# Gated tiles of four feed-forward layers transposed by VectorE in 32 x 32 blocks instead of by TensorE

## The chip, the cores and the metric

One core of a Trainium2 chip. The time is the device time of one execution of the whole program, in microseconds (us). The kernel before was run three times: 1187.49 us median, 1187.45 to 1188.47.

## What is computed

Two transformer blocks in sequence over x of 256 tokens by 1024 features, all in float32. The first has a gated MLP mixer, a feed-forward layer, a chunked attention with relative bias and a second feed-forward layer; the second has a feed-forward layer, a mixer of sparse and stick-breaking attention, a cross attention to a memory, and a feed-forward layer. Four feed-forward layers (f0, f1, f2, f3 in the kernel) are what the change touches. Each is

```python
def _swiglu_ffn(x, g_norm, w_gate_up, w_down):
    h = _rms_norm(x, g_norm)
    gate, up = jnp.split(h @ w_gate_up, 2, axis=-1)
    return (jax.nn.silu(gate) * up) @ w_down
```

with 2816 hidden features, added to x (with factor 0.5 in f2 and f3).

## The kernel before

**Numbers.** Every float32 operand of the large products is kept as two fp32r parts, hi (a rounded copy) and lo (the rest), and a product is three matmuls, hi hi, hi lo, lo hi (helper `three`, L325 to L327).

**Weights.** They come from HBM in units of 128 x 2048 float32 (1 MB). SyncE's queue loads a unit into one of three raw buffers; the load of unit i waits until the unit i-3 has been split. ScalarE copies raw to `whi` (L1069), VectorE subtracts to `wlo` (L1530); the pair goes into one of six slots, and ScalarE waits until TensorE no longer uses the unit that had the slot. Both engines call this `split()`. A chunk takes three units: two of the gate and up weights, one of the down weights, in the order gate-up c (two units), down c-1.

**A feed-forward layer.** The hidden features go in 11 chunks c of 256, the tokens in two halves t of 128. A half chunk (c, t) is:

- TensorE: `project` "gu" (c, t): 24 matmuls of 512 columns into bank `GB[t]`, gate in columns 0 to 255, up in 256 to 511.
- ScalarE `gated`: `sil[t]` = silu(gate) (L1184). VectorE `gated`: `hid[t]` = up * rstd * sil (L1654), 128 tokens x 256 features.
- TensorE `turn_hid`: two transposes of 128 x 128 (L331) of `hid[t]` into PSUM bank `XB[t]`.
- ScalarE `hi` (L1099) and VectorE `lo` (L1589): the transposed tile from PSUM into `hT[t]`, parts hi and lo.
- TensorE `downs` (c, t): 12 matmuls of 512 columns with `hT[t]` as stationary operand, added up in two banks over all chunks.

TensorE's order in chunk c: gu (c, 0), turn (c-1, 1), downs (c-1, 0), gu (c, 1), turn (c, 0), downs (c-1, 1). The first chunk has no downs: gu (0, 0), gu (0, 1), turn (0, 0), gu (1, 0), turn (0, 1), downs (0, 0), gu (1, 1). `downs` (c, 0) waits for the unit of down weights, `downs` (c, t) for `lo` (c, t), and gu (c, t) for `hid` (c-1, t), since it overwrites the bank. After the last chunk come turn (10, 1), downs (10, 0), and the last sums.

VectorE's order (and ScalarE's, with `hi` for `lo`) in chunk c: gated (c, 0), lo (c-1, 1), gated (c, 1), lo (c, 0), then `at_chunk(c, False)`, which makes `counts[c]` splits (3 in most chunks, 4 in chunk 1 of f0, f1 and f3, 1 in chunk 10 of f0, f1 and f2, none in chunk 10 of f3). Behind gated (0, 0), `at_chunk(0, True)` makes `early` splits: on VectorE 1 in f0 and 2 in the others, on ScalarE 1. In f0, f1 and f3 the last of the early splits completes the gate and up weights of chunk 1; in f2 it is the down unit of chunk 0. In f2 `beside` puts more work into the chunks: the memory's keys (scaling the transposed memory in chunks 2 and 3, whose banks TensorE needs back for gu (3, 0) and gu (4, 0); two more splits and the key norms in chunk 4; copies in chunk 6) and the angles in chunk 8; a row scaling `whiten(1)` (L1828) stands ahead of its early splits.

Every engine works its list in program order. The order was written by hand; nothing is planned at run time.

Of the kernel before, what the change touches and what calls it, by code (L numbers as in the profile page):

```python
# [26 lines left out]
class Signals:  # L27
# [13 lines left out]
    def inc(self, name, *key, by=1):  # L41
        sem = self.sem(name)
        if self.counting:
            assert self.owner.setdefault(name, self.engine) is self.engine, name
            self.count[name] = self.count.get(name, 0) + by
            assert (name, key) not in self.value, (name, key)
            self.value[name, key] = self.count[name]
        return sem, by
# [10 lines left out]
    def at(self, name, *key):  # L59
        return self.sem(name), 0 if self.counting else self.value[name, key]  # L60
# [69 lines left out]
def flat(a):  # L130
    return a[:, :, :].rearrange("p a b -> p (a b)")
# [6 lines left out]
def block(nc, io, out):  # L138
    ctx = ExitStack()
    sig = Signals(lambda name: ctx.enter_context(nc.semaphore(name)))  # L140
    at, inc, landed, also = sig.at, sig.inc, sig.landed, sig.also
# [24 lines left out]
    PS = [ctx.enter_context(nc.psum_tensor(f"ps{i}", [128, 512], F32)) for i in range(8)]  # L166
# [8 lines left out]
    def stat(*key, n=1):  # L175

        if key not in columns:
            columns[key] = widths[0]
            widths[0] += n
            assert widths[0] <= 608  # L180
        return stats[:, columns[key]:columns[key] + n]
# [138 lines left out]
    def tensor(e):  # L320
# [8 lines left out]
        def turn(bank, srcs, *key):  # L329
            for i, s in enumerate(srcs):  # L330
                m = e.transpose(PS[bank][:, 128 * i:128 * i + 128], s, ident[:, :])  # L331
            m.then_inc(*inc("turned", *key))
# [176 lines left out]
        def ffn(k, S, before, tail, hook=None, enter=enter):  # L509
            pair = []  # L510

            def first(kts):
                if kts[0] % 4 == 0:
                    pair.append(take())
                project(("gu", S, 0, 0), GB[0], half_of(xT, 0), pair, kts=kts, normed=(S, 0))

            def turn_hid(c, t):
                e.wait_ge(*at("hid", S, c, t))
                if c:
                    e.wait_ge(*at("hidlo", S, c - 1, t))  # L520
                turn(XB[t], [hid[t][:, 128 * i:128 * i + 128] for i in range(2)], "hid", S, c, t)

            def downs(c, t, dn, last=False):
                e.wait_ge(*at("hidlo", S, c, t))
                for h in range(2):
                    m = down_bank(h, DB[t][h], hT[t], dn, range(2), c == 0, last, fresh=t == 0 and h == 0)
                    if last:
                        m.then_inc(*inc("product", "sum", S, t, h))
                if not last:
                    m.then_inc(*inc("product", "down", S, c, t))  # L530
                    if t:
                        used(*dn)

            enter(S, before, tail, first)
            for c in range(FFN_CHUNKS):
                if c > 0:
                    pair = [take(), take()]
                    e.wait_ge(*at("hid", S, c - 1, 0))
                    if hook:
                        hook_free(c, 0)  # L540
                    project(("gu", S, c, 0), GB[0], half_of(xT, 0), pair)
                    turn_hid(c - 1, 1)
                    dn = [take()]
                    downs(c - 1, 0, dn)
                    e.wait_ge(*at("hid", S, c - 1, 1))
                    if hook:
                        hook_free(c, 1)
                project(("gu", S, c, 1), GB[1], half_of(xT, 1), pair, normed=None if c else (S, 1), last=True)
                turn_hid(c, 0)
                if hook:  # L550
                    hook(c)
                if c > 0:
                    downs(c - 1, 1, dn)
            turn_hid(10, 1)
            dn = [take()]
            downs(10, 0, dn, True)
            e.wait_ge(*at("hidlo", S, 10, 1))
            return sums_of_x1(S, DB[1], hT[1], dn, range(2), False, dn)
# [503 lines left out]
    def scalar(e):  # L1062
# [8 lines left out]
        def split(n=1):  # L1071

            for _ in range(n):
                i = next(nth)
                if i == 27:
                    e.wait_ge(*at("product", "mix", 3, 1))
                elif i == 76:
                    e.wait_ge(*at("product", "aq", 3))
                elif i == 163:
                    e.wait_ge(*at("product", "smix", 3))  # L1080
                elif i == 168:
                    e.wait_ge(*at("product", "sum", "m", 1, 1))
                elif slot_before[i] is not None:
                    e.wait_ge(*at("product", "used", slot_before[i]))
                for p in range(len(parts_of(i))):
                    split_part(i, p)
# [11 lines left out]
        def copy(dst, src, name, *key, scale=1.0):  # L1098
            e.activation(dst, src, ACT.Copy, scale=scale).then_inc(*inc(name, *key))  # L1099
# [77 lines left out]
        def ffn(S, at_chunk, second):  # L1177
            def gated(c, t):
                e.wait_ge(*at("product", "gu", S, c, t))
                if c == 0:  # L1180
                    e.wait_ge(*at("pool", "rstd", S, t))
                else:
                    e.wait_ge(*at("hid", S, c - 1, t))
                e.activation(sil[t][:, :], PS[GB[t]][:, 0:256], ACT.Silu, scale=stat("r", S, t)).then_inc(*inc("silu", S, c, t))  # L1184

            def hi(c, t):
                e.wait_ge(*at("turned", "hid", S, c, t))
                if c:
                    e.wait_ge(*at("product", "down", S, c - 1, t))
                copy(flat(hT[t][0]), PS[XB[t]][:, 0:256], "hidhi", S, c, t)  # L1190

            gated(0, 0)
            second()
            at_chunk(0, True)
            for c in range(FFN_CHUNKS):
                if c:
                    gated(c, 0)
                    hi(c - 1, 1)
                gated(c, 1)
                hi(c, 0)  # L1200
                at_chunk(c, False)
            hi(FFN_CHUNKS - 1, 1)

        def attention():
# [267 lines left out]
                scaled_hi("f3", 1, h)  # L1472

        def chunks(early, counts, beside=None):
            def at_chunk(c, start):
                if start:
                    split(early)
                    return
                if beside:
                    beside(c)  # L1480
                split(counts[c])
            return at_chunk

        gmlp()
# [22 lines left out]
        def beside(c):  # L1507
            if c == MEM_CHUNK:
                split(2)
            if c in (2, 3, MEM_CHUNK):  # L1510
                next(keys)
            if c == MEM_CHUNK + 4:
                e.wait_ge(*at("clamped"))
                a = ang[:, :, :, :].rearrange("p a b c -> p (a b c)")
                e.activation(a, a, ACT.Sin).then_inc(*inc("sin"))
# [7 lines left out]
    def vector(e):  # L1523
# [63 lines left out]
        def evac_lo(dst, ps, hi, name, *key):  # L1587
            e.wait_ge(*at(hi, *key))
            e.tensor_tensor(dst[1], ps, dst[0].bitcast(F32), ALU.subtract).then_inc(*inc(name, *key))  # L1589
# [61 lines left out]
        def ffn(S, at_chunk):  # L1651
            def gated(c, t):
                e.wait_ge(*at("silu", S, c, t))
                e.scalar_tensor_tensor(out=hid[t][:, :], in0=PS[GB[t]][:, 256:512], scalar=stat("r", S, t), in1=sil[t][:, :], op0=ALU.mult, op1=ALU.mult).then_inc(*inc("hid", S, c, t))  # L1654

            def lo(c, t):
                evac_lo([flat(a) for a in hT[t]], PS[XB[t]][:, 0:256], "hidhi", "hidlo", S, c, t)

            gated(0, 0)
            at_chunk(0, True)  # L1660
            for c in range(FFN_CHUNKS):
                if c:
                    gated(c, 0)
                    lo(c - 1, 1)
                gated(c, 1)
                lo(c, 0)
                at_chunk(c, False)
            lo(FFN_CHUNKS - 1, 1)

        def rms_rows(S):  # L1670
# [381 lines left out]

        def chunks(early, counts, beside=None):

            def at_chunk(c, start):
                if start:
                    split(early)
                    return
                if beside:
                    beside(c)  # L2060
                split(counts[c])
            return at_chunk

        gmlp()
# [18 lines left out]
            if c == MEM_CHUNK + 4:  # L2083
                mixer_angles()

        def chunk_f2(c, start):
            if start:
                whiten(1)
            chunks(2, [3, *[3] * 9, 1], beside)(c, start)

        ffn("f2", chunk_f2)
        mixer()
# [281 lines left out]
```

## Time and profile before

| | |
|---|---|
| median of three runs | 1187.49 us |
| the profiled execution | 1187.5 us |
| its span, first to last instruction | 1185.7 us |
| TensorE busy | 1175.4 us, 99% |
| VectorE busy | 697.1 us, 59% |
| ScalarE busy | 589.5 us, 50% |
| HBM traffic | 179 GB/s over the span |

The span is the time between the first and the last instruction of the profiled execution; 1.8 us of the device time lie outside it. Busy time of TensorE counts modelled ends of pipelined matmuls, so the distance from start to start tells more than a mean duration. A row of the timeline gives start, duration, engine, line, operation, tile written and tiles read, count, and in brackets the idle time before it with what ended it.

### The profile page before, as it was taken

How to read it: one execution, taken by the hardware profiler on the slowest of the kernel's cores; microseconds unless marked ns; L12 is line 12 of the kernel's file. 1: busy time of each engine (PE TensorE's matmuls, PEld its weight loads, DVE VectorE, ACT ScalarE, POOL GpSimd, SP SyncE). 2: the span in 40 equal slices, each digit the busy share in tenths (PEclk: the TensorE clock that was granted, in tenths of full speed). 3: DMA queues.
4: the chain of work that ended last, by engine and by line, in shares of the span. 5: the costliest groups of instructions: out<-in, count | busy, mean ns of one | idle time of the engine just before them, and what ended most of it. 6: DMA issues, size and time to landing. Idle time of an engine off the chain costs nothing.

```text
span 1185.7 us, 15309 instructions
## 1 busy us (share of the span) xinstructions
PE 1175.4 (99%) x6161; PEld 982.2 (83%) x6161; DVE 697.1 (59%) x958; ACT 589.5 (50%) x797; POOL 59.8 (5%) x109
## 2 busy tenths in 40 slices
PE   9999999999999999999999999999999999999998
PEld 7888888888889988888888888888898877888887
DVE  6666566544557767644555675545568777654452
ACT  7754455443455555543344464434568866544331
POOL 1100010000000000000001500000110002000000
PEclk9999999999999999999999999999999999999999
DMA  7744556445534445645542665455354142754540
GB/s 285 284 160 175 206 185 227 163 180 213 203 118 178 155 135 210 233 160 209 212 174 98 239 232 201 179 196 197 126 219 173 37 149 69 281 203 160 204 142 36
DMA packets 34687, 213.56 MB, mean 180 GB/s; under 512 B 4665, under 2 KB 6841, under 8 KB 10041
## 3 DMA queue, kind: packets, MB, share of 16 engines
q1 hardware_dynamic: 34617, 212.59, 49.2%
q8 instruction: 49, 0.80, 0.3%
q14 instruction: 21, 0.17, 0.0%
HBM read 211.53 MB, written 1.05 MB: 179 GB/s over the span
## 4 chain that ended last, share of the span: by engine, by line
PE 96%; DVE 2%; ACT 1%; DMA 1%; SPq 0%; issue 0%; POOL 0%; DVEq 0%; POOLq 0%
PE ps L325 29%; PE ps L327 29%; PE ps L326 29%; PE ps L331 4%; PE ps L778 1%; DVE wlo L1530 1%; DMA raw<-in_w_v 1%; PE ps L831 1%; PE ps L650 1%; PE ps L630 0%; DVE tmp L1549 0%; ACT xThi L1090 0%; PE ps L753 0%; ACT whi L1069 0%; PE ps L841 0%
## 5 line engine op out<-in xcount | busy, mean ns | idle before, releaser
L1530 DVE TENSOR_TENSOR wlo<-raw,whi 128x2048 fp32r<-128x2048 f32 (+2 forms) x196 | 431.2, 2234 | 111.0 <-ACT whi L1069 111.0
L1069 ACT ACTIVATE whi<-raw 128x2048 fp32r<-128x2048 f32 (+2 forms) x196 | 357.7, 1869 | 50.5 <-DMA raw<-in_w_dn 13.5
L325 PE MATMUL ps<-whi,xThi 128*128 128x512 f32 (+2 forms) x960 | 373.3, 389 | 1.2 <-DVE wlo L1530 0.7
L327 PE MATMUL ps<-whi,xTlo 128*128 128x512 f32 (+2 forms) x960 | 370.9, 386 | 0.0
L326 PE MATMUL ps<-wlo,xThi 128*128 128x512 f32 (+2 forms) x960 | 370.4, 386 | 0.0
L1184 ACT ACTIVATE f_sil<-ps,stats 128x256 f32<-128x256 f32 x88 | 41.5, 471 | 358.7 <-PE ps L327 358.0
L325 PEld LDWEIGHTS ps<-whi,xThi 128*128 128x128 f32 x960 | 180.4, 188 | 38.6 <-DVE wlo L1530 1.6
L327 PEld LDWEIGHTS ps<-whi,xTlo 128*128 128x128 f32 x960 | 180.2, 188 | 36.5
L326 PEld LDWEIGHTS ps<-wlo,xThi 128*128 128x128 f32 x960 | 180.4, 188 | 35.4
L1654 DVE SCALAR_TENSOR_TENSOR f_hid<-ps,stats,f_sil 128x256 f32<-128x256 f32 x88 | 42.4, 481 | 257.9 <-ACT f_sil L1184 257.8
L325 PE MATMUL ps<-whi,f_hThi 128*128 128x512 f32 x352 | 144.8, 411 | 0.0
L327 PE MATMUL ps<-whi,f_hTlo 128*128 128x512 f32 x352 | 138.1, 392 | 0.0
L326 PE MATMUL ps<-wlo,f_hThi 128*128 128x512 f32 x352 | 137.8, 391 | 0.0
L327 PEld LDWEIGHTS ps<-whi,f_hTlo 128*128 128x128 f32 x352 | 66.1, 188 | 14.2
L326 PEld LDWEIGHTS ps<-wlo,f_hThi 128*128 128x128 f32 x352 | 66.5, 189 | 11.4
L325 PEld LDWEIGHTS ps<-whi,f_hThi 128*128 128x128 f32 x352 | 66.2, 188 | 11.0
L2110 POOL TENSOR_SCALAR stats<-stats 128x1 f32<-128x1 f32 (+3 forms) x27 | 14.2, 525 | 649.6 <-ACT junk L1093 577.0
L1090 ACT ACTIVATE xThi<-tmp 128x512 fp32r<-128x512 f32 x32 | 19.9, 629 | 39.1 <-DVE tmp L1549 39.1
L1589 DVE TENSOR_TENSOR f_hTlo<-ps,f_hThi 128x256 fp32r<-128x256 f32 x88 | 36.5, 415 | 2.3 <-ACT f_hThi L1099 2.3
L325 PE MATMUL ps<-xThi,whi 128*128 128x256 f32 x128 | 36.9, 288 | 0.5 <-DVE wlo L1530 0.5
L326 PE MATMUL ps<-xTlo,whi 128*128 128x256 f32 x128 | 36.2, 283 | 0.0
L327 PE MATMUL ps<-xThi,wlo 128*128 128x256 f32 x128 | 36.2, 283 | 0.0
(290 smaller groups left out, 1180.1 us busy)
## 6 DMA issues: line engine op xcount, KB each, us to landing
raw<-in_w_gu SPq DMA_DIRECT2D x88, 1024.0 KB, 5.7
raw<-in_w_dn SPq DMA_DIRECT2D x44, 1024.0 KB, 6.4
raw<-in_w_u SPq DMA_DIRECT2D x8, 1024.0 KB, 6.0
raw<-in_w_ao SPq DMA_DIRECT2D x8, 1024.0 KB, 5.1
raw<-in_w_v SPq DMA_DIRECT2D x6, 1024.0 KB, 4.9
raw<-in_w_bv SPq DMA_DIRECT2D x4, 1024.0 KB, 6.4
raw<-in_w_bk SPq DMA_DIRECT2D x4, 1024.0 KB, 5.4
raw<-in_w_bq SPq DMA_DIRECT2D x4, 1024.0 KB, 5.2
```

Of the source, the lines that this page charges most:

```text
L325: e.matmul(ps, a[0], b[0], start=start, stop=False)
L326: e.matmul(ps, a[0], b[1], start=False, stop=False)
L327: return e.matmul(ps, a[1], b[0], start=False, stop=stop)
L331: m = e.transpose(PS[bank][:, 128 * i:128 * i + 128], s, ident[:, :])
L650: m = e.matmul(ps, a_v[t][:, 256 * g + 64 * j:256 * g + 64 * j + 64], a_pT[j % 2][:, k, :], start=first, stop=last)
L1069: e.activation(dst[:, cs], raw_cols(i, cs), ACT.Copy).then_inc(*inc("whi", i, p))
L1090: e.activation(parts[0][:, 4 * h:4 * h + 4, 128 * t:128 * t + 128], tmp[h][:, :, :], ACT.Copy).then_inc(*inc("xhi", S, t, h))
L1184: e.activation(sil[t][:, :], PS[GB[t]][:, 0:256], ACT.Silu, scale=stat("r", S, t)).then_inc(*inc("silu", S, c, t))
L1530: e.tensor_tensor(lo[:, cs], raw_cols(i, cs), hi[:, cs].bitcast(F32), ALU.subtract).then_inc(*inc("wlo", i, p))
L1589: e.tensor_tensor(dst[1], ps, dst[0].bitcast(F32), ALU.subtract).then_inc(*inc(name, *key))
L1654: e.scalar_tensor_tensor(out=hid[t][:, :], in0=PS[GB[t]][:, 256:512], scalar=stat("r", S, t), in1=sil[t][:, :], op0=ALU.mult, op1=ALU.mult ...
L2110: done(e.tensor_scalar(m, ss, 1.0 / width, EPS, op0=ALU.mult, op1=ALU.add), "mean", S, *key)
```

## The change

The two TensorE transposes per half chunk go, and with them the PSUM bank they wrote. VectorE writes the transposed tile into `sil[t]` (whose content `gated` has just consumed) with sixteen transposing instructions, one for each pair of a 32-token group i and a 32-feature group j; each takes 32 partitions x 2 x 32 elements of `hid[t]` and writes them to another group of 32 partitions of `sil[t]`. `hi` and `lo` read `sil[t]` in SBUF instead of the bank. silu (c, t) now waits for lo (c-1, t).

The order on VectorE and ScalarE changes too: in chunk c it is gated (c, 0) (with its sixteen), lo (c-1, 1), one split if c > 0 and `counts[c]` > 2, lo (c, 0), gated (c, 1) (with its sixteen), then the remaining splits. TensorE's order stays, without the turns.

```diff
 (tensor, ffn)
-            def turn_hid(c, t):
-                e.wait_ge(*at("hid", S, c, t))
-                if c:
-                    e.wait_ge(*at("hidlo", S, c - 1, t))
-                turn(XB[t], [hid[t][:, 128 * i:128 * i + 128] for i in range(2)], "hid", S, c, t)
-                    turn_hid(c - 1, 1)
-                turn_hid(c, 0)
-            turn_hid(10, 1)
 (scalar, ffn)
                 if c == 0:
                     e.wait_ge(*at("pool", "rstd", S, t))
                 else:
-                    e.wait_ge(*at("hid", S, c - 1, t))
+                    e.wait_ge(*at("hidlo", S, c - 1, t))
             def hi(c, t):
-                e.wait_ge(*at("turned", "hid", S, c, t))
+                e.wait_ge(*at("hidT", S, c, t))
-                copy(flat(hT[t][0]), PS[XB[t]][:, 0:256], "hidhi", S, c, t)
+                copy(flat(hT[t][0]), sil[t][:, :], "hidhi", S, c, t)
 (vector, ffn)
             def gated(c, t):
                 ...
+                turn_hid(c, t)
+            def turn_hid(c, t):
+                a, b = (v[t][:, :].rearrange("p (k n) -> p k n", k=2) for v in (hid, sil))
+                e.wait_ge(*at("hid", S, c, t))
+                for i in range(4):
+                    for j in range(4):
+                        m = e.transpose(b[32 * j:32 * j + 32, :, 32 * i:32 * i + 32], a[32 * i:32 * i + 32, :, 32 * j:32 * j + 32])
+                m.then_inc(*inc("hidT", S, c, t))
             def lo(c, t):
-                evac_lo([flat(a) for a in hT[t]], PS[XB[t]][:, 0:256], "hidhi", "hidlo", S, c, t)
+                evac_lo([flat(a) for a in hT[t]], sil[t][:, :], "hidhi", "hidlo", S, c, t)
             gated(0, 0)
-            at_chunk(0, True)
+            at_chunk(0, "first")
             for c in range(FFN_CHUNKS):
                 if c:
                     gated(c, 0)
                     lo(c - 1, 1)
+                    at_chunk(c, "between")
+                lo(c, 0)
                 gated(c, 1)
-                lo(c, 0)
-                at_chunk(c, False)
+                at_chunk(c, "last")
             lo(FFN_CHUNKS - 1, 1)
 (scalar and vector, chunks)
+                ahead = counts[c] > 2 and c > 0
+                if when == "first":
                     split(early)
+                elif when == "between":
+                    split(ahead)
+                else:
+                    if beside:
+                        beside(c)
+                    split(counts[c] - ahead)
```

## Rows read from the trace of the kernel before

**Rows 1.** The page's first part: busy us, share of the span, instructions, per engine.
```profile
PE 1175.4 (99%) x6161; PEld 982.2 (83%) x6161; DVE 697.1 (59%) x958; ACT 589.5 (50%) x797; POOL 59.8 (5%) x109
```
**Rows 2.** A chunk of f0 by windows: stretch, its us, busy us per engine, clock, DMA.
```profile
180.61:197.44 16.83, 16.83 (x78) 13.86 (x76) 10.53 (x9) 8.71 (x9) 0.00 (x0) 1.00 0.69 250
```
**Rows 3.** Groups by form: shapes, count, busy us, mean ns, idle before and releaser.
```profile
L331 PE MATMUL ps<-ident,f_hid 128*128 128x128 f32 x176 | 33.4, 271 | 0.0
L1530 DVE TENSOR_TENSOR wlo<-raw,whi 128x2048 fp32r<-128x2048 f32 x188 | 423.4, 2287 | 105.4 <-ACT whi L1069 105.4
L1530 DVE TENSOR_TENSOR wlo<-raw,whi 128x512 fp32r<-128x512 f32 x4 | 2.8, 688 | 1.5 <-ACT whi L1069 1.5
L1654 DVE SCALAR_TENSOR_TENSOR f_hid<-ps,stats,f_sil 128x256 f32<-128x256 f32 x88 | 42.4, 481 | 257.9 <-ACT f_sil L1184 257.8
L1589 DVE TENSOR_TENSOR f_hTlo<-ps,f_hThi 128x256 fp32r<-128x256 f32 x88 | 36.5, 415 | 2.3 <-ACT f_hThi L1099 2.3
L1775 DVE SCALAR_TENSOR_TENSOR m_ang<-m_cyc,m_ang 128x48 f32<-128x48 f32 x3 | 0.6, 208 | 0.1
```
**Rows 4.** TensorE's timeline, one half chunk of f0: gu, turn, downs, next turn.
```profile
189.02 0.39 PE L325 MATMUL ps<-whi,xThi 128*128 128x512 f32 x1
...
194.24 0.39 PE L327 MATMUL ps<-whi,xTlo 128*128 128x512 f32 x1
194.47 0.38 PE L331 MATMUL ps<-ident,f_hid 128*128 128x128 f32 x2
...
202.88 0.38 PE L331 MATMUL ps<-ident,f_hid 128*128 128x128 f32 x2
```
**Rows 5.** VectorE's timeline in the same chunk.
```profile
195.17 0.48 DVE L1654 SCALAR_TENSOR_TENSOR f_hid<-ps,stats,f_sil 128x256 f32<-128x256 f32 x1 [2.66 <-ACT f_sil L1184]
...
197.25 6.69 DVE L1530 TENSOR_TENSOR wlo<-raw,whi 128x2048 fp32r<-128x2048 f32 x3 [1.26 <-ACT whi L1069]
```
**Rows 6.** VectorE's timeline: three small operations, each waiting for the one before.
```profile
798.13 0.69 DVE L1775 SCALAR_TENSOR_TENSOR m_ang<-m_cyc,m_ang 128x48 f32<-128x48 f32 x3
```
**Rows 7.** Entry of f0: VectorE's timeline.
```profile
158.84 0.48 DVE L1654 SCALAR_TENSOR_TENSOR f_hid<-ps,stats,f_sil 128x256 f32<-128x256 f32 x1 [1.09 <-ACT f_sil L1184]
161.68 2.29 DVE L1530 TENSOR_TENSOR wlo<-raw,whi 128x2048 fp32r<-128x2048 f32 x1 [2.36 <-ACT whi L1069]
...
166.32 6.80 DVE L1530 TENSOR_TENSOR wlo<-raw,whi 128x2048 fp32r<-128x2048 f32 x3 [1.26 <-ACT whi L1069]
```
**Rows 8.** Entry of f0: ScalarE's silu of half chunk (0, 1).
```profile
163.73 0.47 ACT L1184 ACTIVATE f_sil<-ps,stats 128x256 f32<-128x256 f32 x1 [2.09 <-PE ps L327]
```
**Rows 9.** Entry of f1: VectorE's gated (0, 0), ScalarE's silu (0, 1).
```profile
457.71 0.48 DVE L1654 SCALAR_TENSOR_TENSOR f_hid<-ps,stats,f_sil 128x256 f32<-128x256 f32 x1 [1.10 <-ACT f_sil L1184]
...
462.57 0.47 ACT L1184 ACTIVATE f_sil<-ps,stats 128x256 f32<-128x256 f32 x1 [2.05 <-PE ps L327]
```
**Rows 10.** Entry and first chunks of f2: VectorE, ScalarE, TensorE (and its weight loads).
```profile
645.07 0.48 DVE L1654 SCALAR_TENSOR_TENSOR f_hid<-ps,stats,f_sil 128x256 f32<-128x256 f32 x1
647.15 1.29 DVE L1828 SCALAR_TENSOR_TENSOR x<-x,stats,m_gfin 128x1024 f32<-128x1024 f32 x1 [1.60 <-POOL stats L2111]
...
650.08 0.38 PE L331 MATMUL ps<-ident,f_hid 128*128 128x128 f32 x2
...
671.57 1.91 ACT L1069 ACTIVATE whi<-raw 128x2048 fp32r<-128x2048 f32 x1 [6.41 <-DMA raw<-in_w_gu]
...
681.63 0.85 PEld L331 LDWEIGHTS ps<-ident,m_mem 128*128 128x128 f32 x8 [0.20 <-issue]
```
**Rows 11.** End of f0: VectorE after gu (10, 1).
```profile
329.79 0.48 DVE L1654 SCALAR_TENSOR_TENSOR f_hid<-ps,stats,f_sil 128x256 f32<-128x256 f32 x1 [7.33 <-ACT f_sil L1184]
...
331.87 2.29 DVE L1530 TENSOR_TENSOR wlo<-raw,whi 128x2048 fp32r<-128x2048 f32 x1 [1.26 <-ACT whi L1069]
```

More of the change, by code:

```diff
@@ L1198, in ffn @@
                     hi(c - 1, 1)
+                    at_chunk(c, "between")
+                hi(c, 0)
                 gated(c, 1)
-                hi(c, 0)
-                at_chunk(c, False)
+                at_chunk(c, "last")
             hi(FFN_CHUNKS - 1, 1)
@@ L1474, in chunks, with at_chunk @@
         def chunks(early, counts, beside=None):
-            def at_chunk(c, start):
-                if start:
+            def at_chunk(c, when):
+                ahead = counts[c] > 2 and c > 0
+                if when == "first":
                     split(early)
[L1478 to L1481, printed above, removed]
+                elif when == "between":
[4 more added lines that the diff above has]
+                    split(counts[c] - ahead)
             return at_chunk
@@ L1654, in gated @@
                 e.scalar_tensor_tensor(out=hid[t][:, :], in0=PS[GB[t]][:, 256:512], scalar=stat("r", S, t), in1=sil[t][:, :], op0=ALU.mult, op1=ALU.mult).then_inc(*inc("hid", S, c, t))
+                turn_hid(c, t)
[6 more added lines that the diff above has]
+                m.then_inc(*inc("hidT", S, c, t))
             def lo(c, t):
-                evac_lo([flat(a) for a in hT[t]], PS[XB[t]][:, 0:256], "hidhi", "hidlo", S, c, t)
+                evac_lo([flat(a) for a in hT[t]], sil[t][:, :], "hidhi", "hidlo", S, c, t)
             gated(0, 0)
-            at_chunk(0, True)
+            at_chunk(0, "first")
             for c in range(FFN_CHUNKS):
@@ L1664, in ffn @@
                     lo(c - 1, 1)
+                    at_chunk(c, "between")
+                lo(c, 0)
                 gated(c, 1)
-                lo(c, 0)
-                at_chunk(c, False)
+                at_chunk(c, "last")
             lo(FFN_CHUNKS - 1, 1)
@@ L2053, in chunks, with at_chunk @@
         def chunks(early, counts, beside=None):
-            def at_chunk(c, start):
-                if start:
+            def at_chunk(c, when):
+                ahead = counts[c] > 2 and c > 0
+                if when == "first":
                     split(early)
[L2058 to L2061, printed above, removed]
+                elif when == "between":
+                    split(ahead)
+                else:
+                    if beside:
+                        beside(c)
+                    split(counts[c] - ahead)
             return at_chunk
@@ L2084, in beside, with chunk_f2 @@
                 mixer_angles()
-        def chunk_f2(c, start):
-            if start:
+        def chunk_f2(c, when):
+            if when == "first":
                 whiten(1)
-            chunks(2, [3, *[3] * 9, 1], beside)(c, start)
+            chunks(2, [3, *[3] * 9, 1], beside)(c, when)
         ffn("f2", chunk_f2)
```

## The prediction

> **What bounds the kernel now.** The page's first part comes first: TensorE is busy 1175.4 of 1185.7 us, VectorE 59% [rows 1]. The windows say the same of one chunk: TensorE busy for all of its 16.83 us at clock 1.00, VectorE for 10.53 [rows 2]. So a microsecond taken off TensorE counts in full, and one put on VectorE counts once a wait of TensorE ends on it. For that the timelines are read: when VectorE reaches an operation, and when TensorE wants its result.
>
> **Taken off TensorE.** 176 transposes, 88 pairs, 33.4 us of busy time by modelled ends [rows 3]. Starts tell more: gu's 24 matmuls begin at 189.02 and the last at 194.24, 5.22 / 23 = 0.227 us each; from turn to turn it is 202.88 - 194.47 = 8.41 us [rows 4]. The 36 matmuls between take 36 x 0.227 = 8.16, so a pair costs 0.25, and 88 pairs **22.0 us**. All of it is on the path. A chunk without turns takes 16.32.
>
> **Put on VectorE.** 88 x 16 = 1408 transposing instructions of 64 elements a lane. The trace has none. Call T the distance from one's start to the next one's.
> - From below: a 2048-column split takes 2.287, a 512-column one 0.688 [rows 3]: 1.041 ns a column. Three splits in a row take 6.69, so each follows after 2.20, 0.07 more than its columns [rows 5]. If the sixteen overlap so, T = 0.067 + 0.07 = 0.14.
> - From above: an operation of 48 columns takes 0.208 [rows 3], so one of 64 takes 0.225; in a chain where each waits for the last the step is (0.69 - 0.208) / 2 = 0.24 [rows 6], so 0.26 at 64 columns.
>
> I take T = 0.235, next to the duration: each of the sixteen writes another group of partitions than the one before, and a transposer must have read 32 columns before the first comes out, which leaves little to overlap. Sixteen are then 3.76 us.
>
> The Trainium skill (VectorE: DVE Perf Modes, section Two Vector instructions with no wait between them) says an instruction is held until all earlier ones have finished when its input or output starts in another quadrant of 32 partitions than the last one's. That speaks against this change: every one of the sixteen would be held. Every row here keeps one start partition, so no row shows it. By that rule the step is the duration, and the sum goes as below; by the overlap of the splits it goes as in the first rival.
>
> **VectorE's steady chunk.** Gated 0.48 and its wait on itself 0.04, sixteen 3.76, lo 0.34 (0.415 less the overlap), twice; three splits 6.60: 15.84 us of TensorE's 16.32. It fits, with 0.5 to spare. `hi` and `lo` from SBUF cost what they cost from PSUM within 0.05, and ScalarE has slack. The split set between the gatings is not the trouble either. Behind each gating now stand the sixteen, and behind them all lo and the splits. What TensorE wants early in a layer, before VectorE has got ahead, comes late.
>
> **Entry of f0.** gated (0, 0) ends 159.32 [rows 7]; the sixteen to 163.12; the split (raw part ready 161.65) to 165.32, lo (0, 0) 165.66, gated (0, 1) 166.18, sixteen 169.94, the down unit of chunk 0 ends 172.2. TensorE ends gu (0, 1) at 163.7 [rows 8], gu (1, 0) 24 x 0.227 = 5.44 later, 169.15: wait 3.1 (before, that split ended about 168.6). VectorE: two more splits 176.54, gated (1, 0) 177.06, sixteen 180.8, lo (0, 1) 181.2. TensorE, from 172.25 by downs 12 x 0.227 = 2.72 and gu 5.44, wants it at 180.4: 0.8. VectorE has four splits in chunk 1: one 183.4, lo 183.7, gated (1, 1) 184.2, sixteen 188.0, three 194.6, gated (2, 0) 195.1, sixteen 198.9, lo (1, 1) 199.25; TensorE wants it at 181.2 + 16.3 = 197.5: 1.7. After that lo is in time. f0: **5.6**.
>
> **f1 and f3.** Here two splits stand between the gatings of chunk 0, gate and up weights of chunk 1. Gated ends 458.19, gu (0, 1) 462.5 [rows 9]. Sixteen to 461.99, first split 464.25: gu (1, 0) waits 1.7. Second 466.4, lo, gated 467.25, sixteen 471.0, down unit 473.3, wanted at 464.25 + 5.44: 3.6. Then 0.8 and 1.7 as in f0. f1 **7.8**; f3's entry is built alike, **7.8**.
>
> **f2.** Gated ends 645.55; sixteen 649.35; the row scaling, free from 647.15 [rows 10], to 650.56; two splits 654.96, lo, gated 655.8, sixteen 659.6. The down unit is in time here, but lo (0, 1) stands behind three splits, gated (1, 0) and a third sixteen: 670.9. TensorE ends gu (0, 1) about 650.06 and wants it 13.6 later, 663.7: 7.2. The next split waits for its unit (ScalarE 671.57 to 673.48 by its transfer), then VectorE gets to lo (1, 1) at 689.4 for 687.2: 2.2. In chunks 2 and 3 the memory's transposes (0.9 on TensorE) free their bank only when VectorE has scaled them, and that now stands behind gated and sixteen: 697.5 for 693.0, 4.5, and in chunk 3 0.54 + 0.52 + 3.76 + 1.3 = 6.1 behind gu against 0.9 + 2.72: 2.5. The key copies of chunk 6 likewise: 2.3. f2: **18.7**, the least sure of the terms.
>
> **Ends.** After gu (10, 1), whose gated starts 0.5 later, in f0 at 329.79 [rows 11], VectorE needs 0.5 + 0.52 + 3.76 to 4.8, one split to 7.0 and lo to 7.4; TensorE has the downs of two half chunks, 5.44. 2.0 each in f0, f1, f2; in f3 no split, 0.3: **6.3**.
>
> **Sum.** Waits 5.6 + 7.8 + 7.8 + 18.7 + 6.3 = 46.2, less 22.0: +24.2. The profiled execution took 1187.5 (span 1185.7 and 1.8 around it), the median is 1187.49: **1211.7 us, 2.0% slower**. By T = 0.225 or 0.245 it is 3 us less or 4 more; with a spread on f2, the case alone covers 1200 to 1222.
>
> **The rivals.**
> - *The sixteen overlap, T = 0.14: faster.* Sixteen take 2.27. By the same walk: f0 0.2, f1 2.4, f3 2.2, f2 11.2 (2.7, 3.7, 3.0, 1.0, 0.8), ends 1.5, in sum 17.5, less 22.0: 1183. The splits' overlap speaks for it, the changing partitions against. Between the two walks a hundredth of T is worth 3.1 us, so the sign turns at T = 0.157. Chance 0.18.
> - *VectorE becomes the bound in every chunk.* At T = 0.26, the waited chain's step, its chunk is 2 x (0.86 + 4.16) + 6.6 = 16.64, over 16.32 from T = 0.25 on. Waits at the entries grow by 8, the 28 or so steady chunks by 0.3 each, 9: 1229 to 1232. A unit of VectorE's work then moves the end one for one. Chance 0.20.
> - *TensorE's clock falls in the new waits.* Before, the clock is 1.00 (2.4 GHz) in the stretch shown and TensorE has no wait of that size. Now there are about five of over 3 us. At 1.2 GHz a matmul would step by 0.45; if one gu of 5.44 after each ran so, five cost 27 on top, and half of that is likelier: 1225. The Trainium skill (TensorE: Matmul & The Clock Gate, section Why this matters for your kernels) warns of such gaps; no row here has one. Chance 0.12.
> - *The turns were worth less, or the waits overlap with ones there already*, so that it ends within 0.2%: needs T near 0.157, with the first rival's mechanism. Chance 0.04.
>
> **How the numbers follow.** Forecast 0.46; the others 0.54 together. The predicted time is the forecast's, 1212. The range for 8 in 10 takes in the first rival's 1183 and the second's 1232: 1181 to 1232; outside lie T above 0.26 and a clock that falls often. A change within 0.2% (2.4 us) can't be told from none. Faster has the first rival's chance less a little, 0.17; same 0.05; slower 0.78.
>
> **What would show it.** In the trace after: the transposing instructions' step, 0.235 in VectorE's timeline, 3.7 to 3.8 us for sixteen; VectorE busy about 1030 us (697 + 88 x 3.76); half chunks of TensorE 8.16 apart in mid layer; TensorE waiting for wlo (L1530) at 169 in f0 and at f1's and f3's gu (1, 0), and for lo (L1589) in chunks 1 and 2 and at the ends; f2 losing most. Wrong it would be with a step near 0.14 (then no waits in mid layer and a gain), or over 0.25 (then TensorE waits in every chunk), or if granted clock under 1.00 stands beside the waits.

## The result, and the profile after

The changed kernel takes 1242.11 us (median of 4 runs, 1239.69 to 1243.02) against 1187.86 (1187.45 to 1188.47) for the kernel before: a ratio of 1.0453, with a 95% interval of 1.0440 to 1.0467. It is 54 us slower, where 24 were forecast, and outside the range. The profiled execution took 1242.6; its span is 1240.8, 55.1 over the 1185.7 of before.

The page after, busy time per engine:

```profile
PE 1177.3 (95%) x5985; PEld 977.1 (79%) x5985; DVE 1030.3 (83%) x2366; ACT 602.3 (49%) x797; POOL 55.6 (4%) x109
```

Beside [rows 1]: TensorE has 176 matmuls fewer, 22.0 us of work by the half chunk's step, and yet is busy 1.9 longer. So 23.9 us of its busy time are new and are no work. Its idle time rose by 53.2, from 10.3 (1185.7 - 1175.4) to 63.5 (1240.8 - 1177.3). 53.2 + 23.9 - 22.0 = 55.1: longer waits and busy time that is no work (most of it a slower clock, as the filler run below shows), less the turns. VectorE is busy 1030.3, where 1030 was forecast.

The new operation in the groups of the trace (count, busy us, mean ns, idle before), and VectorE's timeline at the entry of f0 (start, us), beside [rows 5, 7]:

```profile
L1658 DVE STREAM_TRANSPOSE f_sil<-f_hid 32x64 f32<-32x64 f32 x1408 | 332.3, 236 | 21.1
```

```profile
158.71 0.48 DVE L1649 SCALAR_TENSOR_TENSOR f_hid<-ps,stats,f_sil 128x256 f32<-128x256 f32 x1 [1.09 <-ACT f_sil L1175]
159.22 3.98 DVE L1658 STREAM_TRANSPOSE f_sil<-f_hid 32x64 f32<-32x64 f32 x16
163.24 2.29 DVE L1525 TENSOR_TENSOR wlo<-raw,whi 128x2048 fp32r<-128x2048 f32 x1
165.45 0.42 DVE L1584 TENSOR_TENSOR f_hTlo<-f_sil,f_hThi 128x256 fp32r<-128x256 f32 x1
165.78 0.48 DVE L1649 SCALAR_TENSOR_TENSOR f_hid<-ps,stats,f_sil 128x256 f32<-128x256 f32 x1
166.29 3.98 DVE L1658 STREAM_TRANSPOSE f_sil<-f_hid 32x64 f32<-32x64 f32 x16
170.30 6.70 DVE L1525 TENSOR_TENSOR wlo<-raw,whi 128x2048 fp32r<-128x2048 f32 x3
```

Each transpose lasts 0.236, and the step is (3.98 - 0.236) / 15 = 0.25. From 158.71 to the last gating of f0 VectorE idles in no place for more than 0.2, and its steady chunk lasts 16.34 for the 16.32 that TensorE needs:

```profile
244.49 0.48 DVE L1649 SCALAR_TENSOR_TENSOR f_hid<-ps,stats,f_sil 128x256 f32<-128x256 f32 x1
...
260.83 0.48 DVE L1649 SCALAR_TENSOR_TENSOR f_hid<-ps,stats,f_sil 128x256 f32<-128x256 f32 x1
```

The first of the three splits at 170.30 is the down unit that TensorE waits for. TensorE's timeline there, and the windows over it (stretch, its us, busy us of PE, PEld, DVE, ACT, POOL, then the granted clock, DMA share and GB/s):

```profile
168.62 0.39 PE L327 MATMUL ps<-whi,xTlo 128*128 128x512 f32 x1
172.74 0.76 PE L325 MATMUL ps<-whi,f_hThi 128*128 128x512 f32 x1 [3.73 <-DVE wlo L1525]
173.30 0.63 PE L326 MATMUL ps<-wlo,f_hThi 128*128 128x512 f32 x1
173.73 0.63 PE L327 MATMUL ps<-whi,f_hTlo 128*128 128x512 f32 x1
...
176.25 0.39 PE L325 MATMUL ps<-whi,f_hThi 128*128 128x512 f32 x1
```

```profile
167.00:171.00 4.00, 2.01 (x9) 1.31 (x7) 3.79 (x15) 1.24 (x2) 0.00 (x0) 1.00 0.57 236
171.00:175.00 4.00, 2.26 (x5) 1.82 (x6) 4.00 (x3) 2.03 (x3) 0.00 (x0) 0.66 0.36 84
175.00:179.00 4.00, 4.00 (x18) 3.29 (x17) 3.88 (x9) 1.48 (x1) 0.00 (x0) 0.92 1.01 416
```

The wait is 3.73 where 3.1 was walked out. After it the matmuls step by 0.43 in place of 0.227, the lower of the clock's two levels (1.2 GHz), and the clock is back by 176.25. There are 11 such places, each behind a wait (the expectation of the filler run below counted 14; the matmul steps show 11). TensorE's long waits in f2:

```profile
686.30 0.79 PE L325 MATMUL ps<-whi,f_hThi 128*128 128x512 f32 x1 [7.55 <-DVE f_hTlo L1584]
...
714.42 0.47 PE L325 MATMUL ps<-whi,xThi 128*128 128x512 f32 x1 [4.41 <-issue]
...
737.64 0.47 PE L325 MATMUL ps<-whi,xThi 128*128 128x512 f32 x1 [4.11 <-issue]
...
804.49 0.77 PE L325 MATMUL ps<-whi,xThi 128*128 128x512 f32 x1 [4.29 <-issue]
...
857.75 0.50 PE L325 MATMUL ps<-whi,f_hThi 128*128 128x512 f32 x1 [3.88 <-DVE f_hTlo L1584]
...
883.75 0.50 PE L325 MATMUL ps<-whi,f_hThi 128*128 128x512 f32 x1 [2.32 <-DVE f_hTlo L1584]
```

Four of the five forecast ones are there (7.2, 4.5, 2.5, 2.3 forecast; 7.55, 4.41, 4.11, 4.29 found), and so is the end. The fifth, for lo (1, 1), is 1.05 at 706.20 where 2.2 was forecast. The one at 857.75 was not forecast. "Issue" stands at the three that wait for the memory's operations (`hook_free`), since the releasing VectorE operation isn't named there.

By layer, from its first silu to its last (us). "Without turns" is before less 22 x 0.25. "Idle" is the length less TensorE's busy time in that window; "busy, no work" is that busy time less the length without turns, which before was all busy; the slower clock is in it, and so is a little at the edges of every wait.

| | before | without turns | after | idle | busy, no work | waits forecast |
|---|---|---|---|---|---|---|
| f0 | 170.95 | 165.45 | 173.34 | 5.3 | 2.6 | 5.6 |
| f1 | 170.92 | 165.42 | 175.51 | 7.3 | 2.8 | 7.8 |
| f2 | 184.81 | 179.31 | 217.84 | 26.3 | 12.2 | 18.7 |
| f3 | 170.99 | 165.49 | 177.05 | 6.7 | 4.8 | 7.8 |

f2 alone holds 33.0 of the 55.1 (217.84 - 184.81).

### The profile page after: what moved, and what is told of

Its sections match the earlier page's. It is cut to its first block, busy times and chain, and to the rows that moved or that the text cites. A ratio compares the mean times of both kernels' runs of the same rounds, so it can differ in the third digit from the quotient of the medians.

```text
span 1240.8 us, 16285 instructions
## 1 busy us (share of the span) xinstructions
PE 1177.3 (95%) x5985; PEld 977.1 (79%) x5985; DVE 1030.3 (83%) x2366; ACT 602.3 (49%) x797; POOL 55.6 (4%) x109
## 3 DMA queue, kind: packets, MB, share of 16 engines
HBM read 211.53 MB, written 1.05 MB: 171 GB/s over the span
## 4 chain that ended last, share of the span: by engine, by line
PE 75%; DVE 18%; issue 2%; ACT 2%; POOL 1%; DMA 1%; SPq 0%; ACTq 0%; DVEq 0%; POOLq 0%
PE ps L325 23%; PE ps L327 23%; PE ps L326 23%; DVE f_sil L1658 8%; DVE wlo L1525 7%; PE ps L331 2%; DVE f_hid L1649 1%; DVE f_hTlo L1584 1%; PE ps L769 1%; ACT whi L1060 1%; PE ps L822 1%; DMA raw<-in_w_v 1%; POOL m_cmask L2174 1%; PE ps L641 1%; DMA raw<-in_w_gu 0%
## 5 line engine op out<-in xcount | busy, mean ns | idle before, releaser
L1060 ACT ACTIVATE whi<-raw 128x2048 fp32r<-128x2048 f32 (+2 forms) x196 | 364.2, 1868 | 237.1 <-PE ps L327 166.9
L325 PE MATMUL ps<-whi,xThi 128*128 128x512 f32 (+2 forms) x960 | 377.0, 393 | 18.9 <-issue 12.8
L1658 DVE STREAM_TRANSPOSE f_sil<-f_hid 32x64 f32<-32x64 f32 x1408 | 332.3, 236 | 21.1
L327 PE MATMUL ps<-whi,f_hTlo 128*128 128x512 f32 x352 | 141.1, 401 | 0.0
L326 PE MATMUL ps<-wlo,f_hThi 128*128 128x512 f32 x352 | 140.9, 400 | 0.0
L1090 ACT ACTIVATE f_hThi<-f_sil 128x256 fp32r<-128x256 f32 x88 | 36.1, 411 | 64.2 <-DVE f_sil L1658 64.2
L2119 POOL TENSOR_SCALAR stats<-stats 128x1 f32<-128x1 f32 (+3 forms) x27 | 11.7, 435 | 696.3 <-ACT junk L1084 615.3
L1584 DVE TENSOR_TENSOR f_hTlo<-f_sil,f_hThi 128x256 fp32r<-128x256 f32 x88 | 37.3, 424 | 1.9 <-ACT f_hThi L1090 0.5
```

Source lines behind the costliest of these rows:

```text
L325: e.matmul(ps, a[0], b[0], start=start, stop=False)
L326: e.matmul(ps, a[0], b[1], start=False, stop=False)
L327: return e.matmul(ps, a[1], b[0], start=False, stop=stop)
L1060: e.activation(dst[:, cs], raw_cols(i, cs), ACT.Copy).then_inc(*inc("whi", i, p))
L1658: m = e.transpose(b[32 * j:32 * j + 32, :, 32 * i:32 * i + 32], a[32 * i:32 * i + 32, :, 32 * j:32 * j + 32])
```

## The experiments

Each ran beside the kernel before on the same chip; ratios are to it, with 95% intervals. In the diffs BY_VECTOR(S, c, t) says who transposes a half chunk: VectorE with the sixteen, or TensorE's turn as before. AHEAD says whether one split stands between the gatings. Both stand for plain edits at the lines of the diff, and both are true everywhere in the changed kernel. Where TensorE turns a chunk, and in the order of before, lo (c, 0) stands behind gated (c, 1) again.

**The price of a transpose.** Every instruction now writes the partition group that it reads. The blocks are then not exchanged between the groups, so this kernel leaves out a part of the work and its output is not the layer's; it is for the time alone:

```
-  e.transpose(b[32*j:32*j+32, :, 32*i:32*i+32], a[32*i:32*i+32, :, 32*j:32*j+32])
+  e.transpose(b[32*i:32*i+32, :, 32*j:32*j+32], a[32*i:32*i+32, :, 32*j:32*j+32])
```

> The changed kernel, but each of the sixteen writes the group of 32 partitions that it reads, so that 12 of 16 follow one with the same groups (the blocks are not exchanged between groups: the output is not the reference's). If an instruction is held because its group of partitions differs from the last one's, 12 steps fall to about 0.14 and 4 stay at 0.25, sixteen take 2.7 us instead of 4.0, and the time falls to 1190 to 1203. If the step of 0.25 is the transposing instruction's own, sixteen stay at 4.0 and the time at 1242.

Measured: 1198.35 us (1195.67 to 1199.40), ratio 1.0085 (1.0070 to 1.0100). And the loops exchanged, which leaves the result as it is:

```
-  for i in range(4):
-      for j in range(4):
+  for j in range(4):
+      for i in range(4):
           m = e.transpose(b[32*j:...], a[32*i:...])
```

> The sixteen with their two loops exchanged: the partition group that is written changes only every fourth instruction, the group that is read changes at each. The same result. Theory (an instruction is held when either its input or its output starts in another group than the one before): a step of 0.25 in all, sixteen in 3.98, 1242 (1239 to 1245). Rival (only the written group holds it): twelve steps of 0.13 and four of 0.25, sixteen in about 2.5, 1198.

Measured: 1243.18 us (1241.97 to 1245.44), 1.0469 (1.0454 to 1.0485). The sixteen at f0's entry, first of the kernel with the groups kept, then of the exchanged loops:

```profile
159.45 2.51 DVE L1658 STREAM_TRANSPOSE f_sil<-f_hid 32x64 f32<-32x64 f32 x16
```

```profile
159.63 3.98 DVE L1658 STREAM_TRANSPOSE f_sil<-f_hid 32x64 f32<-32x64 f32 x16
```

With both groups kept over four instructions, the steps shrink. One set of four and the next one's first, by the rows that remain from each start on (start, us to the end of the sixteen, and how many are left):

```profile
160.71 1.26 DVE L1658 STREAM_TRANSPOSE f_sil<-f_hid 32x64 f32<-32x64 f32 x8
160.88 1.09 DVE L1658 STREAM_TRANSPOSE f_sil<-f_hid 32x64 f32<-32x64 f32 x7
161.00 0.96 DVE L1658 STREAM_TRANSPOSE f_sil<-f_hid 32x64 f32<-32x64 f32 x6
161.13 0.83 DVE L1658 STREAM_TRANSPOSE f_sil<-f_hid 32x64 f32<-32x64 f32 x5
161.33 0.63 DVE L1658 STREAM_TRANSPOSE f_sil<-f_hid 32x64 f32<-32x64 f32 x4
```

In these sixteen, the 12 steps within a group are 0.17, 0.12 and 0.13, 0.14 in the mean, which was the lower bound; the three at a change of group are 0.20 to 0.21, behind instructions that last 0.19 to 0.20. In the sixteen at f0's entry in the changed kernel all 15 steps are 0.24 to 0.26, also before and behind the four of the sixteen that write the group they read (i = j): so it is the change from one instruction to the next that holds, and not the crossing from one group to another. In the changed kernel the group that is read stays for four instructions and the written one changes; with the loops exchanged it is the other way round, and nothing shrinks in either. So a change of one of the two is enough to hold an instruction. That an instruction is then held for the earlier ones to finish is what the Trainium skill says (VectorE: DVE Perf Modes, section Two Vector instructions with no wait between them), for input and output alike; both runs agree with it. 1242 to 1198: the hold costs some 44 us, with the waits and the clock that hang on it.

**The clock.** Dummy matmuls of 512 columns, 188 in all, into a bank that is free stand ahead of 16 long waits, so that TensorE doesn't fall idle; the number at each is fitted to the wait.

```
+  for _ in range(FILL.get((S, where, c, t), 0)):
+      e.matmul(PS[XB[0]][:, :], xT[0][:, 0, 0:128], ..., start=True, stop=True)
   e.wait_ge(*at("hidlo", S, c, t))
```

> The changed kernel, with dummy matmuls of 512 columns put on TensorE just ahead of 16 of its long waits (5 to 30 of them, a little less than each wait lasted), writing to the bank that the removed turns used. If the clock is what made the loss larger than the walk (14 half-clock stretches, TensorE's busy time 24 us higher than the work less the turns), the stretches go and the time falls by 18 to 24 us, to 1218 to 1224. If the waits for VectorE alone are the loss, the fillers do nothing and it stays at 1242, or a little over where a filler outlasts its wait.

Measured: 1232.18 us (1231.96 to 1232.49), 1.0374 (1.0358 to 1.0389), granted clock 0.998 in the mean. The cure worked, and only 10 us came back, half of what the theory of the clock wanted. The same in f0, f1 and f3 alone:

> The changed kernel with dummy matmuls ahead of the long waits in f0, f1 and f3 only (none in f2), so that TensorE's clock stays at 1.00 there. The half-clock stretches there cost TensorE 2.5 + 2.9 + 4.8 = 10.2 us of busy time in the changed kernel. Theory (in these layers VectorE's chain from the entry on sets the end, and a faster TensorE only waits longer): 1239 to 1241, the layers' lengths shorter by under 2 us in all. Rival (the half-clock time is lost one for one): 1232 or less.

Measured: 1240.34 us (1238.95 to 1241.08), 1.0442 (1.0427 to 1.0456). Windows of f0 and f2, first in the changed kernel, then with all the dummies (PE there includes them):

```profile
158.20:331.54 173.34, 168.01 (x733) 137.84 (x732) 167.12 (x410) 78.27 (x77) 0.73 (x2) 0.99 0.54 194
...
658.20:876.03 217.83, 191.53 (x801) 154.92 (x800) 184.42 (x444) 87.09 (x95) 20.52 (x39) 0.94 0.47 170
```

```profile
158.20:331.54 173.34, 171.22 (x753) 140.09 (x751) 166.78 (x409) 78.73 (x77) 0.73 (x2) 1.00 0.54 194
...
656.10:866.90 210.80, 204.49 (x896) 166.97 (x897) 184.49 (x444) 87.17 (x95) 20.57 (x39) 0.99 0.49 176
```

f0 takes 173.34 with the clock at 0.99 and at 1.00 alike: VectorE hands out lo and wlo at the same moments, and a TensorE that is done earlier waits longer. f1 is the same (175.51 and 175.58), f3 gives 1.5 back (177.05 and 175.56), f2 7.0. The clock was not all of the 23.9, though. With all the dummies TensorE is still busy 8.1 over its work (1204.2 - 188 x 0.227 = 1161.5, and the work is 1175.4 - 22.0 = 1153.4), at a clock of 0.998: most of that is the edges of the waits, where the modelled end of the last matmul (0.39 from its start, for a step of 0.227) and a longer first step count. So about 15.8 us were the half clock, an estimate, and they cost 10.6 of span (1240.8 - 1230.2), most of it in f2. It isn't a term that may be added to the waits where VectorE sets the pace.

**The order of the splits.** Before, with the turns on TensorE, and only the split moved between the gatings; and the sixteen, in the order of before:

```
BY_VECTOR = False everywhere, AHEAD as changed     # e3_splits_only
BY_VECTOR = True everywhere, order as before       # e4_old_order
```

> The kernel before (TensorE's transposes) with only the one split per chunk moved between the gatings on ScalarE and VectorE. My account has the split's place as harmless: 1187 to 1189. A rival, that this split holds back lo and gated (c, 1) on VectorE enough to make TensorE wait, would give 1190 or more.

Measured: 1193.39 us (1193.11 to 1193.69), 1.0047 (1.0032 to 1.0062). My figure was wrong and the rival right: 5.7 us more, 5.2 of them in f2 (190.01 for 184.81; f0, f1 and f3 are as before within 0.04). VectorE in chunk 1 of f2, and TensorE there:

```profile
674.09 2.29 DVE L1551 TENSOR_TENSOR wlo<-raw,whi 128x2048 fp32r<-128x2048 f32 x1 [10.07 <-ACT whi L1083]
676.30 0.48 DVE L1675 SCALAR_TENSOR_TENSOR f_hid<-ps,stats,f_sil 128x256 f32<-128x256 f32 x1
```

```profile
676.83 0.44 PE L336 MATMUL ps<-ident,f_hid 128*128 128x128 f32 x2 [3.60 <-DVE f_hid L1675]
```

The split waits 10 us for its unit, with gated (1, 1) behind it, and TensorE waits 3.60 for that; behind the wait its clock falls (0.61 in 676.80 to 680.00).

> The changed kernel with the sixteen, but the old order on both engines: gated (c, 0), lo (c-1, 1), gated (c, 1), lo (c, 0), all splits behind. VectorE then stands idle until gu (c, 1) ends while its work of a chunk is 16.3 us against TensorE's 16.3, so lo (c-1, 1) comes late in every chunk: 1245 to 1275. If the new order is what cost (rival), it comes out under 1238.

Measured: 1274.29 us (1273.08 to 1279.43), 1.0736 (1.0709 to 1.0763). The new order is worth 32 us with the sixteen in. It is two moves at once, the split between the gatings and lo (c, 0) ahead of gated (c, 1), and no run parts them outside f2. By layer the old order costs 11.6, 12.6 and 10.1 in f0, f1 and f3 and is 9.5 shorter in f2. In mid layer VectorE's chunk takes 17.04 where it took 16.34:

```profile
257.73 0.42 DVE L1610 TENSOR_TENSOR f_hTlo<-f_sil,f_hThi 128x256 fp32r<-128x256 f32 x1
258.76 0.48 DVE L1675 SCALAR_TENSOR_TENSOR f_hid<-ps,stats,f_sil 128x256 f32<-128x256 f32 x1 [0.60 <-ACT f_sil L1198]
```

Since the transposed tile lies in `sil[t]`, silu (c, 1) can't start before lo (c-1, 1) has read it; in the old order gated (c, 1) stands right behind that lo, and VectorE waits 0.60 for silu in each of these chunks. And the changed kernel with f2 alone spared the split between:

```
-  ahead = counts[c] > 2 and c > 0
+  ahead = S != "f2" and counts[c] > 2 and c > 0
```

> The changed kernel, with no split between the gatings in f2 alone (all three behind gated (c, 1)); the rest as changed. Theory (a split between the gatings holds gated (c, 1) for a unit that is not there yet, as it cost 5.7 in f2 with the turns on TensorE): 1236 (1232 to 1239), gained in f2's first chunks. Rival (with the sixteen in, the order hardly matters, or the two late splits now hold the next chunk): 1240 to 1246.

Measured: 1236.14 us (1234.37 to 1237.08), 1.0405 (1.0388 to 1.0423); f2 is 211.62 for 217.84. The same 6 us, seen from the other side: TensorE's waits for the memory's operations fall from 4.41, 4.11 and 4.29 to 2.86, 2.83 and 2.52.

**Where the loss sits.** The changed kernel with f2 as before:

```
BY_VECTOR, AHEAD = (S != "f2")                     # e5_f2_tensor
```

> The changed kernel, with f2 alone as before (its turns on TensorE, all splits behind the gatings); VectorE transposes in f0, f1 and f3. Theory (f2's hooks, the memory's scalings, key copies and the third split behind sixteen, are where most is lost): f2 runs in 185 us in place of 217.8, the others stay at 173 to 177, so 1242 - 33 = 1209 (1206 to 1212). Rival (VectorE's total is what counts, and a layer's loss moves to the next): f0, f1, f3 get longer or f2 stays above 190, over 1218.

Measured: 1206.48 us (1205.06 to 1207.24), 1.0157 (1.0142 to 1.0172). f2 takes 184.93, f0 173.36 and f1 175.57 as in the changed kernel. 36 of the 54 us are f2's, with what follows it. Then only the middle of the other three layers, on the kernel before:

```
BY_VECTOR, AHEAD = (S != "f2" and 3 <= c <= 9)     # e8_mid
```

> VectorE transposes, with one split between the gatings, only in chunks 3 to 9 of f0, f1 and f3; chunks 0 to 2 and 10 and all of f2 as before, turns on TensorE. Theory (the loss sits at entries, ends, and f2; in mid layer VectorE's 16.3 just fit under TensorE's 16.32): 42 pairs x 0.25 = 10.5 less than before, 1177 (1175 to 1181). Rival (in mid layer VectorE at 16.3 is itself the bound, so no slack to take the change of hands, waits of 1 to 3 us per layer): 1183 to 1190.

Measured: 1177.56 us (1176.76 to 1180.46), 0.9919 (0.9904 to 0.9934): below both kernels, and 0.8% below the one before, as expected. f0, f1 and f3 take 167.43, 167.38 and 167.44: each 3.5 less than before, which is 14 pairs by 0.25. Its page:

```profile
PE 1165.0 (99%) x6077; PEld 974.6 (83%) x6077; DVE 856.9 (73%) x1630; ACT 595.8 (51%) x797; POOL 60.4 (5%) x109
```

Three tries for more: both halves from chunk 2 on; one half also in chunks 1, 2 and in f2's 3 to 9; one half everywhere in chunks 1 to 9, in the order of before.

```
... and 2 <= c <= 9                                # e12_two_to_nine
... plus t == 0 in chunks 1, 2 and in f2's 3..9    # e9_more
BY_VECTOR = (1 <= c <= 9 and t == 0), old order    # e10_one_half
```

> As e8_mid, from chunk 2 on in place of 3: VectorE transposes both halves, with one split between the gatings, in chunks 2 to 9 of f0, f1 and f3. Theory (chunk 1 has four splits, VectorE has caught up by chunk 2): 48 pairs x 0.25 = 12 off, 1175.6 (1174 to 1178). Rival (VectorE is not ahead at chunk 2 yet, and at 16.35 a chunk never catches up, so each layer waits 1 to 3 us): 1178 to 1186.

> As e8_mid, and beside it VectorE takes the first half (t = 0) of chunks 1 and 2 in f0, f1 and f3 and of chunks 3 to 9 in f2, in the order of before there. Theory (the turns are worth 0.25 each wherever VectorE's operation isn't late; one half a chunk leaves it 2 us of slack): 55 pairs x 0.25 = 13.8 off 1187.6, 1174 (1172 to 1177). Rival (in chunks 1 and 2 and beside the memory's hooks in f2 VectorE is late by more than 0.25 each): 1178 to 1186.

> VectorE transposes only the first half (t = 0) of chunks 1 to 9, in all four layers, all splits and lo in the order of before; the rest is turned by TensorE. VectorE's chunk is then 10.5 + 3.9 = 14.4 of 16.6. Theory (slack in every chunk, nothing late in mid layer): 36 pairs x 0.25 = 9.0 off, 1178.6 (1177 to 1182). Rival (each sixteen delays something TensorE wants, split or lo, in the old order): over 1188.

Measured: 1185.97 us (1184.46 to 1186.63), 0.9984 (0.9975 to 0.9993); 1184.47 (1182.47 to 1186.87), 0.9974 (0.9964 to 0.9984); 1194.82 (1193.77 to 1196.85), 1.0062 (1.0048 to 1.0075). My theory missed all three times, and each came out in its rival's range. VectorE around chunk 2 of f0, first in e8_mid, then in e12_two_to_nine, and TensorE in the latter:

```profile
190.47 2.29 DVE L1551 TENSOR_TENSOR wlo<-raw,whi 128x2048 fp32r<-128x2048 f32 x1 [2.51 <-ACT whi L1083]
192.68 0.48 DVE L1675 SCALAR_TENSOR_TENSOR f_hid<-ps,stats,f_sil 128x256 f32<-128x256 f32 x1
193.08 0.41 DVE L1610 TENSOR_TENSOR f_hTlo<-ps,f_hThi 128x256 fp32r<-128x256 f32 x1
```

```profile
191.01 2.29 DVE L1551 TENSOR_TENSOR wlo<-raw,whi 128x2048 fp32r<-128x2048 f32 x1 [2.54 <-ACT whi L1083]
193.22 0.48 DVE L1675 SCALAR_TENSOR_TENSOR f_hid<-ps,stats,f_sil 128x256 f32<-128x256 f32 x1
193.73 3.99 DVE L1685 STREAM_TRANSPOSE f_sil<-f_hid 32x64 f32<-32x64 f32 x16
197.75 0.42 DVE L1610 TENSOR_TENSOR f_hTlo<-ps,f_hThi 128x256 fp32r<-128x256 f32 x1
```

```profile
198.23 0.50 PE L330 MATMUL ps<-whi,f_hThi 128*128 128x512 f32 x1 [2.27 <-DVE f_hTlo L1610]
```

VectorE has idle time here, but it lies ahead of a split whose unit isn't there. Gated (2, 0) and lo (1, 1) are just in time behind that split; sixteen instructions between them are 3.98 late minus 1.7 of slack: a wait of 2.27, for a half clock after it and for pairs worth 0.25 each. Slack by busy share said 2 us a chunk; in chunk 2 it is 1.7, once. e9_more and e10_one_half lose at the same place, behind the sixteen of chunk 2: TensorE waits 1.83 in f0 in the one and 2.15 in the other. In e10_one_half a wait of 3.42 at the start of f2 (671.49) comes on top.

## Why the prediction was wrong

*Right:* the direction; the turns (a pair 0.25, so 22.0 in all, confirmed by e8_mid's 3.5 a layer); that the sixteen are held, not overlapped; where TensorE would wait, at nearly all of the places walked out; f2 as the layer that loses most; VectorE's busy time. Not found in the trace after is the wait of 0.8 for lo (0, 1) in f0 and f1: TensorE came to it later by its lower clock, and with the dummies it is there (0.74 at 182.32, 0.78 at 487.82). In f3 the wait for the down unit is 1.95 where 3.6 was forecast, since the clock had fallen ahead of it, behind the wait of 2.08 at 1058.97.

*The step that failed is the sum of the waits, its f2 term (18.7) above all; and the forecast left the clock out.* At nearly full clock (e1_fill, 0.998) the span is 1230.2 - 1185.7 + 22.0 = 66.5 over a kernel without turns, so the waits are worth 66.5, not 46.2. By layer, the length there less the length without turns:

| | forecast | e1_fill | off by |
|---|---|---|---|
| f0 | 5.6 | 7.9 | 2.3 |
| f1 | 7.8 | 10.2 | 2.4 |
| f2 | 18.7 | 31.5 | 12.8 |
| f3 | 7.8 | 10.1 | 2.3 |
| ends and the rest | 6.3 | 6.8 | 0.5 |

That is 20.3 of the miss. The clock makes the other 10.6, and together they are the 30.9 between the forecast +24.2 and the +55.1 of the span.

- *T.* Taken 0.235, found 0.25, by the prediction's own slope 4.6 us. It was inside the bounds (0.14 to 0.26); "next to the duration" was right, and the duration is 0.236, but a held step is 0.014 longer than that, as the waited chain of [rows 6] had shown it longer than 0.208.
- *VectorE's steady chunk.* Put at 15.84 of 16.32, "with 0.5 to spare". It is 16.34 (gated (c, 0) at 244.49 and at 260.83 in the trace after), with VectorE idle nowhere for long. So what is late at the entry is never caught up, and most of the clock lost there is hidden behind it. The second rival had this mechanism and put its start at T = 0.25.
- *f2's hooks.* "The split set between the gatings is not the trouble" was wrong by 5 to 6 us there (e3_splits_only, e7_f2_late). I had listed the late unit of [rows 10], 671.57 to 673.48, and charged it to lo (1, 1) alone, not to gated (1, 1) behind it. TensorE waits 4.11 and 4.29 for the scaling in chunk 3 and the key copies, 3.6 more than forecast; without the split between the gatings they are 2.83 and 2.52 (e7_f2_late), so most of the 3.6 is that same split. In chunk 8 `mixer_angles` and the sixteen around it make lo (8, 1) 3.88 late, which the walk didn't have at all: it stopped at chunk 6.
- *The clock.* The third rival had the mechanism ("five cost 27 on top, and half of that is likelier") and a chance of 0.12. [Rows 2] showed the clock at 1.00 only because TensorE never waited. The size of the rival was about right: about 15.8 of busy time, 10.6 of span. The clock fell behind waits down to 1.93 us, in 11 places, not five. The Trainium skill (TensorE: Matmul & The Clock Gate, section Why this matters for your kernels) warns of longer gaps than that; here shorter ones did it too.
- *The form of the rivals.* The second and the third were alternatives to the forecast, each with its price added to it alone. They are not alternatives: both conditions held at once, with more waits in f2, and the range ended where only one of them did (1232).
- *The sign.* The sign was to turn at T = 0.157. e2_same_group has a mean step of (2.51 - 0.20) / 15 = 0.154 and is 10.7 us slower than the kernel before. From there to the changed kernel a hundredth of T is worth (1242.1 - 1198.4) / 9.6 = 4.6 us, clock included, where the two walks gave 3.1. By that slope the sign would turn near 0.13, an estimate, which is below the 0.14 of steps that aren't held; no run reached it. In the middle of three layers the full 0.25 pays.

Open: of the 20.3 of undersized waits, 7.0 lie in f0, f1 and f3, and most of T's 4.6 must be among them; in f2 the split between the gatings makes 5 to 6 and the wait of chunk 8 3.9. The last 3 to 4, in f2 and at the ends, have no run of their own, and the overlaps among all these were not measured apart. Nor was which of f2's waits the 7.0 of its clock belong to.

## What to carry to other kernels

Before work is moved to an engine with 40% to spare, find in its timeline what it idles for: idle time ahead of an operation that waits for data is no slack for what is queued behind it. Move the work only in the stretches where the engine runs ahead of its consumer (here chunks 3 to 9 of three of the layers: 0.8% faster, where the whole move is 4.5% slower). And price TensorE's clock together with each new wait, but add it only where the late engine isn't the one that sets the pace.

## What the runs showed of the hardware

- A VectorE transpose of 64 elements a lane on 32 partitions lasts 0.236 us, and the step to the next is 0.25 when the group of partitions that is read or the one that is written changes from one to the next; when neither does, it is 0.12 to 0.17 (0.14 in the mean). The operations on all 128 partitions around it follow each other 0.07 to 0.09 before the last one's end.
- TensorE at 1.00 dropped to half clock behind single waits of 1.93 to 2.32 us as well as behind those of 3.6 to 7.5, though not behind each of the short ones: not behind 2.14 at 470.51 nor behind 2.32 at 883.75, while the 2.32 at 339.26 did it, and 3 us of half clock followed 1.93 at 1095.98. It lasted 2.5 to 6 us of matmuls, at a step of 0.43 in place of 0.227. In the longest wait it fell before TensorE went on (0.50 in 682.00 to 686.30); behind 1.93 at 1095.98 the slow steps begin only 1.3 us after the wait.
- Dummy matmuls hold the clock: 0.998 for 0.981, worth 10 us of 1242 here.
